# An encoder block on one core: the rest tile's down product with high and low activations in one stationary matrix, and mixer rows written modulated and permuted

## What is computed

```
mod = silu(c) @ w_ada + b_ada                      # six rows of 1024: sh1 sc1 g1 sh2 sc2 g2
...                                                # attention and a short convolution, from x
mixed = concat(rms_norm(attn), rms_norm(conv))
x  = x + g1 * (mixed @ w_out)
h2 = rms_norm(x, norm2_g) * (1 + sc2) + sh2
# mixture of 32 experts (4 groups of 8): a token goes to 2 experts of its best group
logits = h2 @ w_router + b_router
a = silu(h2 @ w_gate[e]) * (h2 @ w_up[e])          # 1024 -> 256
y = a @ w_down[e]                                  # 256 -> 1024
x = x + g2 * sum of gate * y
out = rms_norm(x, final_g)
```

## Time and profile before

| | us |
|---|---|
| timed, median of 3 runs | 1998.89 (1997.29 to 2000.41) |
| profiled execution, its span from first to last instruction | 1996.9 |
| project and attend | 0 to about 1060 |
| mix | about 1060 to 1330 |
| route and the experts' tables | about 1330 to 1378 |
| experts | about 1378 to 1952 |
| combine | about 1952 to 1997 |

### The profile page before, as it was taken

One profiled execution on the slowest core, in us unless ns is written; L12 is line 12 of the kernel. 1 busy time (PEld: TensorE's weight loads), 2 busy tenths in 40 slices (PEclk: granted clock), 3 DMA queues, 4 the chain that ended last, 5 costly groups with the idle time before them and its releaser, 6 DMA issues. The chain is left out here.

```text
span 1996.9 us, 26921 instructions
## 1 busy us (share of the span) xinstructions
PE 1804.3 (90%) x8987; PEld 1482.5 (74%) x8988; DVE 1181.1 (59%) x2015; ACT 854.9 (43%) x1520; POOL 855.0 (43%) x887
## 2 busy tenths in 40 slices
PE   2999999997999999999995999965999999999970
PEld 2777878764777777777784788854999988888960
DVE  4687889956766766666645555553444444444434
ACT  3535454326777677667684132311222222222214
POOL 0132314103888888888892111122243434434330
PEclk9999999996999999999996999977999999999995
DMA  7656555530000000000006344415899998999948
GB/s 282 197 164 185 172 163 165 147 95 0 6 9 6 9 9 6 11 7 6 11 11 218 105 157 141 143 43 189 278 268 276 279 276 270 278 276 274 272 91 336
DMA packets 216176, 291.05 MB, mean 146 GB/s; under 512 B 24373, under 2 KB 172048, under 8 KB 215834
## 3 DMA queue, kind: packets, MB, share of 16 engines
q1 hardware_dynamic: 193498, 220.60, 33.3%
q0 software_dynamic: 20224, 69.22, 13.9%
q10 hardware_dynamic: 2368, 0.17, 0.1%
HBM read 229.13 MB, written 60.82 MB: 145 GB/s over the span
## 5 line engine op out<-in xcount | busy, mean ns | idle before, releaser
L1212 POOL TENSOR_TENSOR plo<-KR,phi 128x512 fp32r<-128x512 f32 (+1 forms) x320 | 352.3, 1118 | 44.8 <-ACT KR L1171 44.6
L1020 DVE TENSOR_REDUCE cmax<-tbank 128x1 f32<-128x512 f32 (+2 forms) x320 | 193.4, 605 | 106.4 <-PE tbank L835 101.2
L1170 ACT ACTIVATE phi<-tbank 128x512 fp32r<-128x512 f32 (+1 forms) x320 | 170.7, 533 | 141.6 <-PE tbank L884 137.1
L387 PE MATMUL pbank<-hhi,wslhi 128*128 128x512 f32 x512 | 207.9, 406 | 6.7 <-DVE wsllo L440 6.7
L1946 DVE TENSOR_SCALAR xTe<-ebank,modcol 128x256 f32<-128x256 f32 (+1 forms) x128 | 53.7, 472 | 258.9 <-PE ebank L1864 137.6
L387 PE MATMUL pbank<-hhi,wsllo 128*128 128x512 f32 x512 | 201.9, 394 | 0.0
L387 PE MATMUL pbank<-hlo,wslhi 128*128 128x512 f32 x512 | 201.9, 394 | 0.0
L331 POOL DMA_DIRECT2D wmod<-in_w_ada x64 | 48.4, 757 | 305.2 <-DVE macc L519 295.2
L1886 PE MATMUL ebank<-xTe,wg 128*128 128x192 f32 x1024 | 171.8, 326 | 3.1 <-DVE ahi L1974 1.8
L1886 PEld LDWEIGHTS ebank<-xTe,wg 128*128 128x128 f32 x1024 | 167.9, 190 | 7.9 <-DVE ahi L1974 2.1
L1886 PE MATMUL ebank<-xTe,wu 128*128 128x192 f32 x1024 | 171.6, 326 | 0.0
(11 more groups left out here) (283 smaller groups left out, 3976.8 us busy)
## 6 DMA issues: line engine op xcount, KB each, us to landing
wg<-in_w_exp_gate SPq DMA_DIRECT2D x32, 1024.0 KB, 5.9
wu<-in_w_exp_up SPq DMA_DIRECT2D x32, 1024.0 KB, 9.0
wd<-in_w_exp_down SPq DMA_DIRECT2D x32, 1024.0 KB, 7.6
wraw<-in_w_in SPq DMA_DIRECT2D x60, 512.0 KB, 4.2
wmod<-in_w_ada POOLq DMA_DIRECT2D x64, 256.0 KB, 3.4
xt<-in_x SPq DMA_DIRECT2D x4, 2048.0 KB, 12.7
wada<-in_w_ada SPq DMA_DIRECT2D x4, 2048.0 KB, 18.7
mixed<-mix_dram SPq DMA_DIRECT2D x16, 512.0 KB, 4.3
```

The source lines that it names most:

```text
L387: ins = pe.matmul(out, w[:, S % 3, k], h[:, n % 2, k], start=k == 0 and j == 0, stop=k == KD - 1 and j == 2)
L1020: W(ve.tensor_reduce(cmax[:, i % 2, n:n + 1], plain[:, chunk % 2, 0:w], AX.X, ALU.max), plain_read)
L1170: A(act.activation(step_of(phi, m), scores[:, m % 2, j * P:512], ACT.Exp), phi_done)
L1212: po.tensor_tensor(step_of(plo, m), step_of(probs, m), step_of(phi, m).bitcast(F32), ALU.subtract).then_inc(plo_done, 1)
```

## The change

In `mix`, `xs` becomes the finished row h2, in permuted order. DVE's last step of a tile is now a product of three factors, x times 1/rms times a row `scrow` = norm2_g * (1 + sc2), with x read at a step of 8 elements, so that feature p*8 + k stands at place k*128 + p. GpSimd then adds the row `shrow` (sh2, permuted) in place (`shift`), and only that sets `xs_ready`, for which the store and the transposes wait. `scrow` and `shrow` are made once, in the first tile's step, from three rows that SP loads (1.5 MB into all partitions) and from two more pairs of `modulation_rows`; the narrow products L1411 and L1418, `wrs` and the bias step go. The router's weights are loaded in the permuted order, (p k).

In `experts`, the gate and up weights are loaded in the same order: 8 KB in a piece for a partition, where before there were eight pieces of 1 KB. The copies from PSUM are plain copies, one instruction in place of two or four. High and low activations lie in one tensor `aa`, so that the 64 high and the 64 low columns of the rest tile form one stationary matrix of 128; the product with `dhi` gives high x high in partitions 0 to 63 and low x high in 64 to 127. `down_rest` has 8 products in place of 12. ACT copies the low half to `yb` (`low_rest`), DVE adds the high half, then scales: three steps in place of one.

```
-                ve.tensor_scalar(xs[:, b], x2[:, b], xstat[:, b, 2:3], None, ALU.mult).then_inc(xs_ready, 1)
+                ve.scalar_tensor_tensor(chunks(xs[:, b]), by_chunk(x2[:, b]), xstat[:, b, 2:3], chunks(scrow[:]),
+                                        ALU.mult, ALU.mult).then_inc(x_scaled, 1)
...
+        def by_chunk(ap):
+            return ap.rearrange("p (j k) -> p k j", k=KD)
...
+            def shift(t, b):
+                hold(po, x_scaled, t + 1, passed_pool)
+                po.tensor_tensor(xs[:, b], xs[:, b], shrow[:], ALU.add).then_inc(xs_ready, 1)
...
                 if at == 0:
                     sum_squares(0, 0)
                     modulation_rows(0, 0)
+                    pe.wait_ge(mod_read, 1)
+                    modulation_rows(1, 4)
...
-                    pe.wait_ge(mod_read, 1)
-                    modulation_columns()
+                    pe.wait_ge(mod_read, 2)
+                    modulation_rows(1, 2)
                 if at == 1:
-                    router_shift()
                     pe.wait_ge(mod_read, 4)
...
-                if at == 1:
-                    pe.wait_ge(rbias_read, 1)
...
+            def modulation():
+                spread = turn.rearrange("p a n -> p (a n)")
+                ve.wait_ge(ld_rows, 16 * 3)
                 ve.wait_ge(mod_summed, 2)
+                ve.tensor_tensor(scale_in, scale_in, spread, ALU.add).then_inc(mod_read, 1)
                 ve.wait_ge(mod_read, 2)
+                ve.scalar_tensor_tensor(chunks(scrow[:]), by_chunk(scale_in), 1.0, by_chunk(gain_in), ALU.add, ALU.mult)
+                ve.wait_ge(mod_summed, 3)
+                ve.tensor_tensor(chunks(shrow[:]), by_chunk(shift_in), by_chunk(spread), ALU.add).then_inc(mod_read, 1)
...
-            wgd = T["w_exp_gate"].rearrange("l e (k p) n -> p (l e k) n", p=P)
+            wgd = T["w_exp_gate"].rearrange("l e (p k) n -> p (l e) (k n)", k=KD)
...
             def down_rest(q, b, r):
-                pe.wait_ge(yb_done, r * NEXP + q * 2 + (b + 1))
-                down(outb, b, 0 if b else P, CAPB if b else CAP, down_b)
+                pe.wait_ge(rest_read, r * NEXP + q * 2 + (b + 1))
+                def both_parts(f):
+                    for n in range(2):
+                        ins = pe.matmul(outb[:, n], aa[:, b, f, BOTH], dhi[:, b, f, n * 512:(n + 1) * 512],
+                                        start=f == 0, stop=f == KF - 1)
+                    return ins
+                def high_part(f):
+                    for n in range(2):
+                        pe.matmul(outb[0:CAPB, n], aa[:, b, f, REST], dlo[:, b, f, n * 512:(n + 1) * 512],
+                                  start=False, stop=False)
+                both_parts(0)
+                high_part(0)
+                high_part(1)
+                both_parts(1).then_inc(down_b, 1)
...
+            def low_rest(q, b, r):
+                act.wait_ge(st_yb[b], r * (PAIRS * 16) + q * 16)
+                act.wait_ge(down_b, r * NEXP + q * 2 + (b + 3))
+                act.activation(yb[:, b], outb[CAPB:P].rearrange("p a n -> p (a n)"), ACT.Copy).then_inc(low_copied, 1)
```

More of the change, by code:

```diff
@@ L1319, in _ @@
             load_macc(1, slice(2, 6))
+            b = T["b_ada"]
+            for row, src in ((scale_in, b[0, 4 * D:5 * D]), (gain_in, T["norm2_g"][0, :]), (shift_in, b[0, 3 * D:4 * D])):
+                sp.dma_start(row, src.partition_broadcast(P)).then_inc(ld_rows, 16)
             load_x(1, 1)
@@ L1366, in route @@
             def route(t, b):
+                if isinstance(t, int) and t == 0:
+                    pe.wait_ge(ld_r, 16 * 4)
                 pe.wait_ge(x_copied, t + 1)
@@ L1406, in modulation_rows @@
                 ins.then_inc(mod_summed, 1)
[L1408 to L1419, removed]
             tiles(pe, step)
@@ L1549, in step @@
                     mixers_in(t + 1, 1 - b)
+                if not last:
+                    act.wait_ge(m_reduced, t + 2)
                 act.wait_ge(x2_ready, t + 1)
-                act.activation(junk[:], x2[:, b], ACT.Square, accum_out=xstat[:, b, 0:1]).then_inc(x2_squared, 1)
+                act.activation(junk, x2[:, b], ACT.Square, accum_out=xstat[:, b, 0:1]).then_inc(x2_squared, 1)
                 act.wait_ge(x2_step, t * 2 + 2)
@@ L1579, in _ @@
                 for b in range(2):
+                    shift(i * 2 + b, b)
                     step(i * 2 + (2 + b), b)
+            shift(NT - 2, 0)
+            shift(NT - 1, 1)
 def route(nc, T, st):
@@ L1888, in gate_up @@
                     ins.then_inc(done, 1)
[L1890 to L1896, removed]
             def down_first(q, b, r):
@@ L1901, in down_first @@
                 pe.wait_ge(ya_done, r * NEXP + q * 2 + (b + 1))
-                down(outa, b, b * CAPB, b * CAPB + P, down_a)
-            def down_rest(q, b, r):
-                pe.wait_ge(yb_done, r * NEXP + q * 2 + (b + 1))
-                down(outb, b, 0 if b else P, CAPB if b else CAP, down_b)
+                for f in range(KF):
+                    for j, (h, w) in enumerate(((HIGH, dhi), (LOW, dhi), (HIGH, dlo))):
+                        for n in range(2):
+                            ins = pe.matmul(outa[:, n], aa[:, b, f, h], w[:, b, f, n * 512:(n + 1) * 512],
+                                            start=f == 0 and j == 0, stop=f == KF - 1 and j == 2)
+                ins.then_inc(down_a, 1)
+            def down_rest(q, b, r):
+                pe.wait_ge(rest_read, r * NEXP + q * 2 + (b + 1))
[5 more added lines that the diff above has]
+                def high_part(f):
+                    for n in range(2):
+                        pe.matmul(outb[0:CAPB, n], aa[:, b, f, REST], dlo[:, b, f, n * 512:(n + 1) * 512],
[4 more added lines that the diff above has]
+                both_parts(1).then_inc(down_b, 1)
             pe.sem_inc(turned, 6)
@@ L1995, in _ @@
             ve.sem_inc(yb_done, 1)
+            ve.sem_inc(rest_read, 1)
             ve.sem_inc(ya_done, 1)
@@ L2122, in _ @@
                 split_down(PAIRS - 1, 1, r)
+                for b in range(2):
+                    low_rest(PAIRS - 1, b, r)
 def combine(nc, T, st, out):
```

116 lines of the change are left out of this document (56 added, 60 removed).

## The result

The changed kernel takes 2010.32 us (median of 4 runs, 2008.74 to 2011.96), the kernel before 1998.09 (median of 4) in the same comparison. The ratio is 1.0059, with a 95% interval from 1.0045 to 1.0073: slower by 12 us. The profiled span is 2008.9 us where it was 1996.9, so the two traces differ by +12.0.

The account below looks back on a forecast made before the run. TensorE was taken to bound both stages, in mix with a chain through ACT's copy. Terms -27.6 - 1.8 + 1.1 - 0.9 + 0.8 + 17.3 + 16.5 = +5.4 us gave 2004 us, range 1983 to 2012.

Parts of the forecast that it names:

- The expert loop: Rest tile's down product: four fewer products save 0.92 us an expert, new DVE and ACT work is covered; -27.6 us.
- the rival of bound transfers: Expert loop: DMA transfers bind, so half of the 27.6 us saving is lost; 2018 us, chance 0.04.
- The xs step: Steady tiles of mix: DVE's longer three-factor step with strided read adds 1.33 us a tile, +17.3 us over 13.
- Rival 2: Mix: the strided read costs nothing, TensorE idles 0.6 us a tile; 1977 us, chance 0.16.
- The clock: Steady tiles of mix: idle time before narrow router products lowers TensorE's clock, 1.65 us in 10 tiles; +16.5, bounds 0 and 21.
- Rival 1: Mix: the clock holds, so the 16.5 us drops out; 1988 us, chance 0.27.
- Rival 4: Mix: DVE's reciprocal of `mstat` is held while GpSimd shifts, 2.4 us a tile, +28 us; 2032 us, chance 0.03.
- The head of mix: Start of mix: 3.7 us idle, more rows and a clock fall against narrow products removed; -0.9 us, give or take 4.
- The start of the experts: Start of the expert stage: plain copies replace two by one and four by one; -1.8 us.
- the end of the experts: Last experts: rest tile ready later by ACT's copy and DVE's sum, less savings; +1.1 us.
- the three signs: Whole kernel against 1998.89 us: faster (below 1994.9) 0.44, within 0.18, slower (above 2002.9) 0.38.
- the forecast's own case: Mix: the clock falls in 5 to 13 tiles, whole kernel 1996 to 2010 us; chance 0.50.

Follow-up runs that it names:

- Experiment 3: The kernel before with only the rest tile's new down product (8 products in place of 12, ACT's copy, DVE's sum and scaling): 1970.35 us, ratio 0.9862.
- experiment 2: The changed kernel without the permutation: x read in a row, router's and experts' weights loaded in the old order: 1978.42 us, ratio 0.9905.
- experiment 1: The changed kernel with ACT's copy of the transposed row moved ahead of its root for the next mixers in mix: 1963.8 us, ratio 0.9829.
- experiment 4: The changed kernel with six useless dense products in each mix tile from tile 2, ahead of the router product: 1987.91 us, ratio 0.9949.
- experiment 5: The changed kernel with 6 of the second half's 24 dense products put between TensorE's wait and the router product: 1987.87 us, ratio 0.9948.

## Why the prediction was right or wrong

**The expert loop** was right to a tenth: 0.92 us an expert, no wait of TensorE, the new DVE and ACT steps covered. Experiment 3 shows it alone. That the rival of bound transfers was out is seen twice: at a share of 0.99 in experiments 2 and 3 TensorE doesn't wait, and with the weights in pieces of 8 KB the share is 0.93 at 291 GB/s.

**The xs step** was right: 1.42 us a tile on the path where 1.33 was said, taken from L1431 and L1697. That the size came out so close is in part luck: the price was read from another instruction at a step of 128 elements, and no run varies the step. Rival 2 (the strided read is free) is out by experiment 2, in which the xs step differs only in the order of the addresses. The Trainium skill, SBUF — State Buffer, section "Door 1: The DMA port swizzle", by which an access that crosses to a new line pays, leans the same way; the figure, 1.28 against 2.17 us for 1024 elements read at a step of 8, is this case's.

**The clock** was right as a mechanism and too small. The prediction's argument was one stretch of the trace with idle time and narrow products, and one with idle time and dense work. Experiments 1, 4 and 5 take away the idle time, fill it, and put dense work behind it, and each time the clock holds. The term was mis-sized at both of its factors: the fall came in 12 of 13 tiles where 10 were taken, and in three of them it lasted twice as long, 3.3 us where 1.65 was taken for every fall. The upper bound of 21 us was therefore none: it rested on a single stretch at the lower clock as if all were as long. The kernel before already had a longer one. Behind the first fall of the earlier trace rows its clock stayed down for some 10 us, the last 3.5 of them in dense products (TensorE alone):

```profile
1089.00:1098.50 9.50, 9.50 (x37) 0.50 0.50 179
```

Measured: 24.7, which is 8.2 more than said and more than the whole 6.7 us by which the sum was short.

**Rival 1**, the clock holds, decides at four falls or fewer, and there were twelve. Experiments 4 and 5 are this rival made real, at 1988 us, the time that it was given.

**Rival 4**, the reciprocal held while GpSimd shifts, is out. (Its price was also summed wrongly: 13 tiles at 2.4 us are 31 us, not 28.) The reciprocal of the mixers' scale in the changed kernel:

```profile
L1439 DVE RECIPROCAL mstat<-mstat x16: 165/165/167, 1082.0 to 1344.5; 128x2 f32<-128x2 f32 x16
```

**The head of mix** was 2.2 us better than said, in this pair of traces. The forecast had 3.7 us of idle time ahead of the second pair of rows, and a fall of the clock behind it. TensorE idled only 1.73 us there, since its first products had run longer at the lower clock and its first pair of rows ended at 1083.00, and the clock held: the products from 1086.99 on take 0.62 for two. The forecast's case came in experiment 2, where the same wait was 4.04 us. Its second pair of rows, and a window of TensorE behind the wait:

```profile
1085.05 3.62 PE L1419 MATMUL mbank<-macc_all,cst 128*128 128x512 f32 x4 [4.04 <-DMA macc_all<-mod_dram]
```

```profile
1085.00:1088.00 3.00, 2.95 (x5) 0.50 1.03 411
```

There the clock fell, although the products behind the wait are dense (512 columns). In the other four kernels with this head the wait was 1.73 to 2.60 us, the same rows took 1.96, and the clock held. So the step that failed is the length of the wait, and dense products behind a wait keep the clock up for waits of 1.4 to 2.6 us in these runs, not for one of 4.04. (In the earlier trace rows the clock fell behind a wait of 2.93 us ahead of dense products, with narrow work before the wait.) The size of the gain is loose as well. From mix's first dense product to tile 2's xs step it is 62.9, 59.7, 62.8 and 61.6 us in the four kernels with the old head, and 58.8 to 60.5 in the five with the new one.

**The start of the experts** came out at +0.6 in place of -1.8. The quicker copies gave 1.5 of the 1.8. But the first gate group took 7.44 us until the next, before 5.30, since the clock rose later. In experiment 1, whose copies are the same, the clock rose in time, and the stretch from the first transpose to the second expert's gate group took 17.00 us where the kernel before has 18.83: the -1.8 of the forecast. In the nine traces this group took 5.3 us six times and 6.96 or 7.44 three times. The three are among the five kernels with the plain copies, none among the four with the old ones. It can be chance, or come of the group starting earlier; that stays open.

**What was missing altogether** is the step from the last logits to the first transpose, -2.05 us: TensorE's wait for the first gathered rows is 7.38 us and was 9.30. In the five kernels with small weight pieces that wait is 8.9 to 10.0 us, in the four with pieces of 8 KB it is 6.9 to 8.1. Experiment 2, the changed kernel with small pieces, has 10.04. The prediction looked at the layout of the weights for the loop alone.

**The time**: +5.4 was said and +12.1 measured; 2010 lies in the range, near its end. The difference is what is left of errors both ways: the clock, the xs step and the experts' start were 11.8 us too low together (8.2 + 1.2 + 2.4), the head of mix, the missing step and the end of the experts 5.1 too high. So the number is better than its terms. Of the three signs the largest chance, 0.44, was put on faster, and slower, which came, had 0.38; the forecast's own case, 5 to 13 falls, was the likeliest, and it came with 12.

## What to carry to other kernels

A step that gets longer is dear or free by what stands between it and the engine that bounds the stage. Here one line of order on ACT turned a loss of 12 us into a gain of 35 (of which 29 are the down product's), because the copy that TensorE waited for didn't need the long step at all: when an operation of the chain is lengthened, look which of the steps queued behind it can pass.

When TensorE waits, look at what it does first when it wakes. Idle time of 1.4 us ahead of 1.8 us of narrow products cost as much again and more in clock (1.9 us a tile) as in waiting; with 1.5 us of dense products first it cost nothing extra. That held for waits up to 2.6 us here; behind one of 4.04 us dense products ran at the lower clock too. And when the length of an effect is read from one stretch, that stretch is a size, and no upper bound.

## What the runs showed of the hardware

- A three-factor DVE step over 1024 elements of 4 bytes takes 1.28 us with all reads in a row, and 2.17 with one of them at a step of 8 elements (2.08 to 2.28 over the runs).
- The changed kernel is 22 us faster with six useless products in each tile than without them.
- In the last tile a DVE sum of two SBUF rows took 2.00 us in place of 1.23, while GpSimd's shift of 2.36 us ran over its start:

```profile
1344.87 2.36 POOL L1578 TENSOR_TENSOR xs<-xs,shrow 128x1024 f32<-128x1024 f32 x1 [12.86 <-DVE xs L1466]
1346.30 2.00 DVE L1449 TENSOR_TENSOR x<-x,xin 128x1024 f32<-128x1024 f32 x1
```

  The same happened in the last tile of all five kernels with the shift (2.00 to 2.04 us, and 1.60 in experiment 2, where less of the shift was left), and never in the kernel before, which has no shift (1.22 to 1.23). The Trainium skill, SBUF — State Buffer, section "SBUF: two separate sides", says that a DVE step with two inputs from SBUF and a GpSimd step that reads SBUF exclude each other for a port pair. The traces agree: in all five the sum begins beside the shift and ends 1.07 or 1.08 us behind the shift's end. The step ahead of it, which has one input from PSUM (L1446), ran beside the shift too and took its usual 1.28.
